# Two blocks of a transformer on one core: order of the tail's steps behind a norm, and where the modulation's column sums stand

## The reference, cut to what matters

```
f = swiglu(rms_norm(h, ln_ffn1[i, 0]), ffn1_w_gu[i], ffn1_w_down[i])
h = h + 0.5 * rms_norm(f, ln_ffn1[i, 1])
hn = rms_norm(h, ln_mix[i, 0])
m = short_conv_mixer(hn, ...)        # layer 0;  diff_attention_mixer in layer 1
h = h + rms_norm(m, ln_mix[i, 1])
f = swiglu(rms_norm(h, ln_ffn2[i, 0]), ffn2_w_gu[i], ffn2_w_down[i])
h = h + 0.5 * rms_norm(f, ln_ffn2[i, 1])
...
mod = silu(c) @ w_mod + b_mod        # second block: 6 vectors of 1024, one row of c
```

## Time and profile before

| | |
|---|---|
| median of 3 runs | 1457.52 us (1456.22 to 1459.17) |
| profiled execution, its own time | 1455.59 us |
| its span | 1453.7 us |
| PE busy | 1435.6 us (99%) |
| DVE busy | 1048.0 us (72%) |
| ACT busy | 701.0 us (48%) |
| PE's waits for x_lo (L1471) | 1.7 us, 6 times |
| PE's waits for x_hi (L2253) | 3.1 us, 4 times |

### The profile page before, as it was taken

One profiled execution on the slowest core, in us unless ns is written; L12 is line 12 of the kernel. 1 busy time (PEld: TensorE's weight loads), 2 busy tenths in 40 slices (PEclk: granted clock), 3 DMA queues, 4 the chain that ended last, 5 costly groups with the idle time before them and its releaser, 6 DMA issues. The chain is left out here.

```text
span 1453.7 us, 28394 instructions
## 1 busy us (share of the span) xinstructions
PE 1435.6 (99%) x11582; PEld 1397.1 (96%) x11582; DVE 1048.0 (72%) x1423; ACT 701.0 (48%) x910; POOL 28.9 (2%) x58
## 2 busy tenths in 40 slices
PE   9999999999999999999999999999999999999999
PEld 8999999999999999999999989999987899999999
DVE  6766779777667786667787668767887777786542
ACT  6544344355444354443454656444445766564441
POOL 0000100000000000001000000000000000000000
PEclk9999999999999999999999999999999999999999
DMA  9555745426556835547543225647832435455550
GB/s 330 221 187 188 254 167 203 174 88 261 175 181 219 291 128 204 181 181 264 183 162 114 75 88 206 229 181 244 292 135 93 172 131 219 173 192 197 202 192 30
DMA packets 42540, 269.11 MB, mean 185 GB/s; under 512 B 4768, under 2 KB 5920, under 8 KB 13520
## 3 DMA queue, kind: packets, MB, share of 16 engines
q1 hardware_dynamic: 33984, 240.31, 45.7%
q0 software_dynamic: 7312, 26.44, 5.5%
q10 hardware_dynamic: 1152, 1.05, 0.2%
HBM read 266.73 MB, written 1.05 MB: 184 GB/s over the span
## 5 line engine op out<-in xcount | busy, mean ns | idle before, releaser
L422 PE MATMUL ps<-x_hi,w_hi 128*128 128x272 f32 (+2 forms) x2040 | 590.2, 289 | 4.3 <-DVE x_lo L1471 1.7
L423 PE MATMUL ps<-x_lo,w_hi 128*128 128x272 f32 (+2 forms) x2040 | 580.6, 285 | 0.0
L424 PE MATMUL ps<-x_hi,w_lo 128*128 128x272 f32 (+2 forms) x2040 | 580.6, 285 | 0.0
L2109 ACT ACTIVATE w_hi<-raw_weights 128x2048 fp32r<-128x2048 f32 x219 | 416.7, 1912 | 287.7 <-PE ps L424 285.1
L1210 DVE TENSOR_TENSOR w_lo<-raw_weights,w_hi 128x2048 fp32r<-128x2048 f32 x193 | 439.5, 2288 | 142.6 <-ACT w_hi L2109 142.1
L422 PEld LDWEIGHTS ps<-x_hi,w_hi 128*128 128x128 f32 x2040 | 385.5, 189 | 8.1 <-DVE x_lo L1471 2.5
L423 PEld LDWEIGHTS ps<-x_lo,w_hi 128*128 128x128 f32 x2040 | 385.6, 189 | 0.7
L424 PEld LDWEIGHTS ps<-x_hi,w_lo 128*128 128x128 f32 x2040 | 385.3, 189 | 0.0
L422 PE MATMUL ps<-a_hi,w_hi 128*128 128x272 f32 x592 | 169.9, 287 | 0.0
L424 PE MATMUL ps<-a_hi,w_lo 128*128 128x272 f32 x592 | 169.9, 287 | 0.0
L423 PE MATMUL ps<-a_lo,w_hi 128*128 128x272 f32 x592 | 169.9, 287 | 0.0
(11 more groups left out here) (271 smaller groups left out, 1892.0 us busy)
## 6 DMA issues: line engine op xcount, KB each, us to landing
raw_weights<-w_units SPq DMA_DIRECT2D x226, 1024.0 KB, 4.9
mod_w<-mod_units POOLq DMA_DIRECT2D x48, 512.0 KB, 5.6
raw_weights<-w_units SPq DMA_DIRECT2D x4, 256.0 KB, 5.3
raw_weights<-w_units SPq DMA_DIRECT2D x2, 512.0 KB, 8.3
out<-h ACTq DMA_DIRECT2D x8, 128.0 KB, 1.8
h<-x_in SPq DMA_DIRECT2D x2, 272.0 KB, 4.0
h<-x_in SPq DMA_DIRECT2D x1, 544.0 KB, 6.8
tab<-tables POOLq DMA_DIRECT2D x1, 512.0 KB, 5.7
```

The lines of the kernel that those rows point to most:

```text
L422: pe.matmul(dst, wh, hi, start=start, stop=False)
L423: pe.matmul(dst, wh, lo, start=False, stop=False)
L424: return pe.matmul(dst, wl, hi, start=False, stop=stop)
L2109: act.activation(w_hi[:, u % RING, :], raw[:, u % RING, :], ACT.Copy).then_inc(S["hi_ready"], 1)
```

## The change

Two edits. In the five tails DVE's order in step m (from m = 2) becomes: L1454 of m, L1471 of m-1, L1466 of m, add of m-2. In three of them (into conv_in, up 2, qkv) six of the twelve modulation sums are made in `stats`, each with one filler behind it, after two fillers and a wait for ACT's copies of f (`f_kept`, since the sums' bank held tile 6 of the old stage); the other six stand behind k = 5, 6 and 7, two each. The number of fillers stays 8.

```diff
+EARLY_SUMS = 6
...
-            def stats(st, nx, evict=True, filler=8):
+            def stats(st, nx, evict=True, filler=8, part=None):
...
                 spread(nx.T, spread_bank(nx))
-                keep_busy(st, filler)
+                if evict:
+                    c.up("f_kept", KT - COPIED)
+                if part is None:
+                    keep_busy(st, filler)
+                    return
+                keep_busy(st, 2)
+                pe.wait_ge(S["f_kept"], c.now("f_kept"))
+                for n in range(EARLY_SUMS):
+                    mod_sums(part, mod_bank(nx), range(n, n + 1))
+                    keep_busy(st, 1)
...
                     for k in range(COPIED, KT):
-                        job = (lambda columns: lambda: mod_sums(part, mod_bank(st), columns))(
-                            range(4 * (k - COPIED), 4 * (k - COPIED) + 4))
+                        first = EARLY_SUMS + 2 * (k - COPIED)
+                        job = (lambda columns: lambda: mod_sums(part, mod_bank(st), columns))(range(first, first + 2))
...
+                def low_part(k):
+
+                    if 0 <= k < 8:
+                        dve.wait_ge(S["x_hi_ready"], c.up("x_hi_ready"))
+                        dve.scalar_tensor_tensor(lo[:, k, 0:T], h[:, k, off:off + T], next_gain[:, k:k + 1],
+                                                 hi[:, k, 0:T].bitcast(F32), ALU.mult, ALU.subtract)\
+                           .then_inc(S["x_ready"], 1)
+
...
-                    if m >= 2 and nx is not None:
+                    low_first = deferred and normed and m >= 2
+                    if low_first:
+                        low_part(m - 1)
+                    elif m >= 2 and nx is not None:
                         add_square(m - 2, T, last)
...
-                    k = m - 1
-                    if 0 <= k < 8 and deferred:
-                        dve.wait_ge(S["x_hi_ready"], c.up("x_hi_ready"))
-                        dve.scalar_tensor_tensor(lo[:, k, 0:T], h[:, k, off:off + T], next_gain[:, k:k + 1],
-                                                 hi[:, k, 0:T].bitcast(F32), ALU.mult, ALU.subtract)\
-                           .then_inc(S["x_ready"], 1)
+                    if low_first:
+                        add_square(m - 2, T, last)
+                    elif deferred:
+                        low_part(m - 1)
```

More of the change, by code:

```diff
@@ L751, in _ @@
             conv = stages["conv_in"]
-            stats(stages["down", 0], conv)
+            stats(stages["down", 0], conv, part=0)
             first_groups(conv, X0["conv_in"], 0)
@@ L760, in _ @@
             k_outer(stages["down", 1], (a_hi, a_lo), A0["up", 1])
-            stats(stages["down", 1], stages["up", 2])
+            stats(stages["down", 1], stages["up", 2], part=1)
             gate_up(2, X0["up", 2], 1)
@@ L765, in _ @@
             qkv = stages["qkv"]
-            stats(stages["down", 2], qkv)
+            stats(stages["down", 2], qkv, part=2)
             def bank7_free():
```

## The result

The change makes the kernel slower: a median of 1464.99 us against 1457.45, a ratio of 1.0054 (95% interval 1.0030 to 1.0077), which is 7.9 us (4.4 to 11.2). I had forecast slower with 0.71 and put +5.15 us on it. Three single executions of 2679 to 2876 us (one of the kernel before, one of the changed kernel, one of a variant) are left out of every ratio.

What follows compares the result with a forecast made beforehand. PE bounds the kernel, busy 99% of the span, following DVE in the tails. Lags of 0.8 + 0.8 + 0.8 + 1.25 + 1.5 = 5.15 us, clock 0, give 1462.7 us, 0.35% more; range 1458.0 to 1465.2.

Steps and rivals of the forecast that it cites:

- What bounds the kernel: Whole kernel: PE is busy 99% of the span; in the tails it follows DVE's x_lo from k = 1 on.
- Part 2: DVE's new order in the tails: the add delays square, x_hi[3] and x_lo[3]; DVE leaves 1.3 us late.
- Where the lag meets PE: PE's meetings with late DVE: conv_in, up 2 and up 1 +0.8 us each, qkv +1.25, up 3 +1.5.
- Part 1: Six sums fewer behind k = 5 to 7 give PE 1.2 us in each of three stages.
- That costs nothing: PE starting k = 0 some 0.4 us late is hidden, as x_lo[1] and x_lo[2] come 0.5 us earlier.
- The clock ... I take 0 for both: Falls in three tails, 0 to +1.1 us each, and at most 0.5 us back in conv_in: both taken as 0.
- 1 (no detour): Tails: the detour on ACT through the square doesn't bite; +1.4 us, 1458.9; chance 0.08.
- 2: Tile 2 of the second group: PE doesn't meet the sums' late eviction; -0.85 us, 1456.7; chance 0.09.
- rival 3: Tails: the early x_lo feeds PE alone, 0.66 us in each of five; -6.9 us, 1450.6; chance 0.06.

Runs made afterwards that it cites:

- the early eviction: Sums moved, and DVE evicts the modulation sums right behind the reciprocal: 1.0008 with x_hi[3] ahead of the square, 1.0001 with DVE's old order, against the kernel before.
- the filled kernels: The whole change plus filler matmuls ahead of qkv's first rotation: 1.0064 with 24, 1.0039 with 12, against the kernel before.

## What the prediction had right, and the step that failed

- *What bounds the kernel, and Part 2.* Right in every step: the square that waits for the first add, x_hi[3] behind it, x_lo[3] no earlier than before, h 0.9 late, DVE 1.4 late at the end of the tail and 1.2 at L1380 (1.3 and 1.25 worked out). Shown by the rows and by putting x_hi[3] ahead of the square.
- *Where the lag meets PE.* Tile 2 in conv_in and up 2 (1.69 us of stand in up 2 for the 1.9 worked out), the row sums of up 1, the first evictions in qkv, w_lo in up 3: each wait is in the trace. Free of falls, conv_in, up 1, up 2, qkv and up 3 grew by 0.8, 1.0, 0.8, 1.2 and 1.6 us against 0.8, 0.8, 0.8, 1.25 and 1.5. In up 3 the row sums wait as well (0.67 us), which I had not named.
- *Part 1.* The early sums win 1.2 us as far as L1380: shown by the early eviction (up 2 1.3 us shorter). "That costs nothing" holds without the clock alone, see the next point.
- *The step that failed is "The clock ... I take 0 for both".* I bounded falls in the three tails with moved sums (0 to 1.1 each) and put them at nothing, and left out the place where my own steps put PE's longest stand: 0.7 from before, 1.2 of gained sums, 1.2 of lag make 3.0 us in qkv. The runs show in place of the 0:
  - In qkv the clock fell with the stand in 4 of 4 traces that have it at 3.0 us (the changed kernel's three, and the one with x_hi[3] ahead), in 1 of 6 with a stand of 1.7 to 1.95 us, and not with 12 fillers in it. It cost 1.4 to 1.5 us, and 2.8 where it was double. This brings the sum to 6.6.
  - In conv_in's tail the changed kernel had a double fall in all three traces, which cost 0.3 to 0.7 us against the traces of the filled kernels without it. This brings the sum to some 7, against 7.9 measured, or 7.5 by the medians.
  - A long stand is not needed for a fall. The Trainium skill ("TensorE: Matmul & The Clock Gate", the section on HAM oscillation) describes a kernel whose clock falls again and again because PE waits too long between bursts of matmuls; I had weighed it only where it promised a gain. The four falls with the stand of 3.0 us agree with it in kind. By the measurements a much shorter stand can go with a fall as well: ahead of up 3 PE stands only 1.55 us for the squares, in the old order and in the new, and a fall came within 3 us behind it in 9 of 16 traces, at a price of 0 to 0.6 us.
- *A term was missing altogether.* The matmuls of a whole stage may run at a longer step, 4.9 us in up 1 with down 1 and 6.0 in up 3 with down 3. It was there from the tail on in 2 of 11 traces with the new order in up 1's tail and in 4 of 11 with it in up 3's, and in none of the five each with the old order there. With the order in up 3 alone, 6 of 12 timed runs lay at 1463 us or more. With the lag of 1.6 us taken off, that is 1461.5, and 12 of 75 runs of the kernel before lay there, 6 of the 23 run in between. So such slow runs are not new with the change, and that its waits raise their share is possible but not shown.
- *Rivals.* 1 (no detour) was wrong by the rows, and so were 2 and 3. The kernel built nearest to rival 3 (x_hi[3] ahead and the early eviction) was not shown to be faster than the kernel before either.
- *What is open.* The order alone loses as much as the whole change, though its lags add up to 4.9 us and no fall stands behind its wait in qkv; one of its three traces has the 6 us of the slower step. So the lag of DVE is shown, and the price of the falls in the changed kernel's traces, but how the rest of the loss in the timed runs is made up of falls and slower steps is not, and neither is why the step settles at one or the other value.

## What to carry to other kernels

Before a step is put ahead of another on one engine, follow the buffer that the displaced step frees: here a late add held a square, the square held the next input on an in-order engine, and the early step waited for that input. Work moved out of PE's list ahead of a wait only makes the wait longer, and a long stand can cost a second time, through the clock. Where the runs of a kernel spread by 0.5%, one trace isn't the kernel: take three, compare them stage by stage, and look at the spread of the kernel before as well.

## What the runs showed of the hardware

- With equal code and full granted clock, matmuls of 272 columns with their weight loads start every 123.3 or 126.7 ns (up 1 in the second and in the first trace of the changed kernel), those of 256 every 113.3 or 117.8 ns (up 3 in its second and in its third). The value changed behind a longer step between two starts: 0.94 us at the row sums of up 1, but also 0.24 us at the start of down 3 (at 1011 us in its first trace, where no idle time shows). Then it held for 60 to 190 us.
- Each fall of the clock before the last matmuls took 3.4 us or 6.8 in all 16 traces. What this costs depends on what PE does then: 0.5 us for a single one in conv_in's tail, where PE has time to spare (kernel before), 1.3 us in the tail behind down 3 (its second trace), and 1.4 to 1.5 us in qkv (changed kernel).
- Single-column fp32 matmuls among the fillers go with more time at half clock: mean clock 0.995 in the 11 runs with the sums alone against 0.998, and double falls in the tails of 8 of 9 traces with moved sums against 0 of 7.
